# A hybrid attention and retention layer on one core: all values projected first, the pairs' turns written out and overlapped

## The chip, the cores and the metric

The kernel runs on 1 core of one Trainium2 chip. The metric is device time in microseconds (us); the kernel before takes 620.38 us, median of 3 runs (620.24 to 620.57). Engines are named as in the profile: PE (TensorE) with its weight loads PEld, DVE (VectorE), ACT (ScalarE), POOL (GpSimd), and SP, which only issues DMAs here.

## The reference, cut to what matters

```python
h = rmsnorm(x, norm_mix_pre)                        # x: 512 tokens x 1024
proj = h @ w_in                                     # columns qa ka va qr kr vr gr, 512 each
ya = moba_attention(qa, ka, va, rel_bias)           # 8 heads of 64: causal softmax, relative bias
yr = retention(qr, kr, vr, gr)                      # 8 heads of 64: rotary, decay, group norm, gate
x = x + rmsnorm(concat(ya, yr) @ w_out, norm_mix_post)
h = rmsnorm(x, norm_ffn_pre)
u = causal_conv3(h @ w_up)                          # 2 x 2816 columns
x = x + rmsnorm((gelu(u_gate) * u_value) @ w_down, norm_ffn_post)
```

With 512 tokens, blocks of 256 and three blocks allowed, the sparse attention is plain causal attention; retention is computed as scores times a decay mask times values, followed by a normalisation over each head's 64 columns and a gate.

## The kernel before, in words

All matrix products are made of three passes (high by high, high by low, low by high): a weight block of 512 KB is loaded into one of four slots of `raw`, ACT copies it to the high part in `ws` (`split_hi`), DVE subtracts for the low part (`split_lo`; POOL for the first block), and PE uses it. `unit_done` frees a slot. A unit of the input projection is 24 matmuls of 512 columns: 128 output columns (a pair of heads) for all tokens, with the weights stationary, into one bank of PSUM.

The mixer works through four pairs of heads. A turn (`mixer_turn`) projects seven units, kA, qA, vA, kR, qR, vR and gR, each in three steps of eight matmuls, and hangs the attention work between the steps: in the first nine steps (r = 0 to 8) the retention scores of the pair before (`ret_scores`), then in twelve steps (u = 0 to 11) the scores, turned probabilities and products of this pair's softmax attention (`moba_scores`, `moba_turn`, `moba_mix`), and the retention mix and group norm of the pair before (`ret_mix`, `ret_rows`, `ret_turn_out`). Turn 0 is written out with its first two units in halves of 256 tokens, turns 1 to 3 are a loop on every engine, and the retention of the last pair lies inside the output projection (`out_rows`).

Values come out of the projection as columns. ACT copies them to SBUF (`evacuate`, backwards in token order), PE transposes them in four 128 x 128 pieces (`moba_values` L801, `ret_values` L751), and ACT copies the rows out again.

Every engine works through its own list in order; a wait on a semaphore holds what is behind it. The lists that matter here, by function:

- ACT: `exponent` (L1225), `swap_halves` (four copies of 32 rows, L1175), `stack_hi` (L1158, L1160), `split_hi` (L1105), `copy_turned` (L1217), `ret_copy`, squares of the centred rows (L1245).
- DVE: `bias_and_max` (L1648), `normalise` (L1655, L1657), `ret_decay` (L1596), `rotate` (L1666, L1667), `stack_lo` (L1577, L1579), `ret_center` (L1608 to L1612), `ret_variance` (L1617), `ret_norm` (L1621), `ret_gate` (L1626), `ret_low`, `gate_finish`, `split_lo` (L1528).
- POOL: for each pair the bias and decay tables' loads, `double_keys` (L634), `group_rstd(i - 1)` (L620 and the power L622), `rotary_sum(i, 0)` and `(i, 1)` (L626).
- PE: every three-pass matmul has the line of the helper `three`, L694; row transposes L705, the warm-up L723.

In the tail, the x rows 0 and 1, whose space held probabilities, are loaded again before the residual is added; x rows 2 and 3 stay in place. `norm_mix_post` has its half of `gains` from the start; `vA` and `vR` lie in the other half, which `norm_ffn_pre` gets later. The feed-forward part (up projection, convolution and down projection, both with seven products instead of eight for blocks) follows.

Of the kernel before, what the change touches and what calls it, by code (L numbers as in the profile page):

```python
# [36 lines left out]
P = 128  # L37
# [12 lines left out]
GROUPS = [1, 0, 2, 4, 3, 5, 6]  # L50
KA, QA, VA, KR, QR, VR, GR = range(7)
NU = 7
OUT0 = NU * PAIRS
# [78 lines left out]


# [68 lines left out]
def at_turn(f, n, i, per_turn):  # L202

    if isinstance(i, int):
        return f(n + i * per_turn)
    a, b = f(n + per_turn), f(n + 2 * per_turn)
    return (b - a) * i + (2 * a - b)


# [5 lines left out]
def build(nc, x, norm_mix_pre, w_in, rel_bias, w_out, norm_mix_post, norm_ffn_pre, w_up,  # L215
          conv_w, conv_b, w_down, norm_ffn_post, rotary, decay, onehot, out):
    ctx = ExitStack()
    with ctx:
# [46 lines left out]
        vA = gains[:, 0, 0:SEQ]  # L265
        vArow = part(0, 512).rearrange("p (t c) -> p t c", t=ST)
        probs = xs[:, 0:2, :].rearrange("p s (r c) -> p (s r) c", c=SEQ)
        probsT = [part(128 + 1664 * h, 2048).rearrange("p (t c) -> p t c", t=ST) for h in range(2)]
        vR = gains[:, 0, SEQ:2 * SEQ]
        vRrow = part(4096, 512).rearrange("p (t c) -> p t c", t=ST)  # L270
        gate = part(4608, 512)
# [89 lines left out]
        UNIT_BANK = [0, 1, 0, 1, 0, 1, 7]  # L361
        S_BANK, T_BANK, YA_BANK, YR_BANK = (2, 3), (4, 5), 6, 7
        O_BANK = [(0, 1), (5, 6), (2, 3), (4, 7)]
        H_BANK = [(2, 3), (4, 5), (6, 7), (2, 3)] + O_BANK
        UP_BANK = [(0, 1, 5, 6), (2, 3, 4, 7)]
        X_BANK, Y_BANK = [(0, 1), (2, 3), (4, 5)], [6, 7]

# [24 lines left out]
        load_granted, bias_granted = sem("load_granted"), sem("bias_granted")  # L392
# [10 lines left out]
        ident_set = sem("ident_set")  # L403
# [10 lines left out]
        evacuated = sem("evacuated")  # L414
# [4 lines left out]
        vA_turned, vA_ready = sem("vA_turned"), sem("vA_ready")  # L419
# [3 lines left out]
        vR_turned, vR_ready = sem("vR_turned"), sem("vR_ready")  # L423
# [64 lines left out]
        def _(sp):  # L488
# [3 lines left out]
            def load(n, i, per_turn, source, k_major=True):  # L492
                c = slot_of(n)
                if not (isinstance(i, int) and freed_at(n + i * per_turn) == 0):

                    m = n if isinstance(i, int) else n + per_turn
                    last_unit = freed_at(m + (i * per_turn if isinstance(i, int) else 0)) - 1
                    sp.wait_ge(lo_sem(last_unit), at_turn(lambda k: lo_count(freed_at(k) - 1), n, i, per_turn))
                    if not isinstance(i, int):
                        sp.sem_inc(load_granted, 1)  # L500
# [5 lines left out]
            def load_turn(i, j0=0, j1=NU):  # L506
                for j in range(j0, j1):
# [1596 lines left out]
```

## Time and profile before

| | |
|---|---|
| median of the runs | 620.38 us |
| runs | 620.57, 620.38, 620.24 us |
| profiled execution, first to last instruction (its span) | 619.2 us |
| median less that span | 1.2 us |
| mean granted clock | 0.995 |
| PE, PEld busy | 98%, 86% |
| DVE, ACT, POOL busy | 77%, 59%, 23% |

The profiled execution comes with its span alone; the 1.2 us between it and the median are what a run has around its instructions. A matmul's busy time overlaps the next one's, so a busy share of PE tells little, and the distance between two starts is what counts. In the timeline an "x8" row is eight instructions of one form in a row, its first number their start and its second the time until the last one has drained.

### The profile page before, as it was taken

Reading aid. Unit: us, or ns where it says so; the run is one execution under the profiler, and the core shown is the slowest. Engines: PE = TensorE matmul, PEld = TensorE weight load, DVE = VectorE, ACT = ScalarE, POOL = GpSimd, SP = SyncE. Lnnn points to the kernel's source line nnn. Section 1 sums busy time; section 2 is a strip of 40 time slices with the busy share of each in tenths; the row PEclk is TensorE's granted clock in tenths of the full one; section 3 lists DMA queues with packets and bytes.
Section 4 is the critical chain, followed back from the end, with each engine's and each line's share of the span. In section 5 each row is a group of like instructions: output and inputs, shape, how many; then the busy total and the mean of one; then the engine's idle time right before and its main releaser. Section 6 shows DMA issues by size and latency. Waiting matters only on the chain.

```text
span 619.2 us, 9966 instructions
## 1 busy us (share of the span) xinstructions
PE 606.9 (98%) x3710; PEld 532.1 (86%) x3710; DVE 473.9 (77%) x678; ACT 365.0 (59%) x571; POOL 143.9 (23%) x145
## 2 busy tenths in 40 slices
PE   8999999999999999999999999999999999899996
PEld 8888778778787877889989999999999988688885
DVE  3657548656855885978975598888999898999886
ACT  5558338536743853773844566666667655766661
POOL 4313103111310302312021222222222223422213
PEclk9999999999999999999999999999999999899999
DMA  9834223322422254681477988998899879996933
GB/s 275 241 105 127 80 69 103 102 67 68 135 68 68 102 193 157 190 242 35 103 168 145 179 169 163 218 185 177 151 224 192 174 145 180 165 223 168 238 93 136
DMA packets 87785, 93.27 MB, mean 151 GB/s; under 512 B 3049, under 2 KB 72345, under 8 KB 87746
## 3 DMA queue, kind: packets, MB, share of 16 engines
q0 software_dynamic: 26352, 35.15, 33.7%
q1 hardware_dynamic: 61394, 57.59, 29.3%
q8 instruction: 25, 0.41, 0.3%
q14 instruction: 14, 0.11, 0.1%
HBM read 90.62 MB, written 2.12 MB: 150 GB/s over the span
## 4 chain that ended last, share of the span: by engine, by line
PE 84%; DVE 8%; POOL 2%; issue 2%; ACT 2%; DMA 1%; DVEq 0%; SPq 0%; POOLq 0%; ACTq 0%
PE bank L694 75%; PE bank L774 1%; PE bank L836 1%; DVE ws L1940 1%; PE bank L705 1%; DMA gains<-in_norm_mix_pre_dram 1%; POOL grstd L622 1%; PE bank L825 1%; DVE xs L1648 1%; PE bank L765 1%; PE bank L764 1%; POOL work L626 1%; PE bank L815 1%; PE bank L814 1%; DVE work L1818 1%
## 5 line engine op out<-in xcount | busy, mean ns | idle before, releaser
L694 PE MATMUL bank<-hT,ws 128*128 128x256 f32 (+1 forms) x1656 | 295.3, 332 | 0.7 <-DVE work L1626 0.6
L694 PEld LDWEIGHTS bank<-hT,ws 128*128 128x128 f32 x1656 | 245.8, 190 | 28.2 <-issue 2.5
L694 PE MATMUL bank<-yT,ws 128*128 128x256 f32 x864 | 106.8, 283 | 0.0
L694 PEld LDWEIGHTS bank<-yT,ws 128*128 128x128 f32 x864 | 105.2, 192 | 0.2
L694 PE MATMUL bank<-ws,yT 128*128 128x512 f32 x366 | 88.0, 396 | 2.3 <-DVE yT L1916 2.3
L694 PEld LDWEIGHTS bank<-ws,yT 128*128 128x128 f32 x366 | 68.9, 191 | 17.0 <-issue 3.1
L1367 ACT ACTIVATE ws<-raw 128x1024 fp32r<-128x1024 f32 x46 | 48.7, 1059 | 46.1 <-PE bank L694 46.1
L1824 DVE TENSOR_TENSOR ws<-raw,ws 128x1024 fp32r<-128x1024 f32 x46 | 56.1, 1220 | 15.2 <-ACT ws L1367 15.2
L1528 DVE TENSOR_TENSOR ws<-raw,ws 128x1024 fp32r<-128x1024 f32 x47 | 57.5, 1224 | 5.8 <-ACT ws L1105 5.4
L669 POOL DMA_DIRECT2D raw<-in_w_up_dram x27 | 34.7, 1284 | 108.1 <-DVE ws L1824 103.6
L1105 ACT ACTIVATE ws<-raw 128x1024 fp32r<-128x1024 f32 x48 | 50.7, 1058 | 14.8 <-PE bank L694 10.8
L694 PE MATMUL bank<-ws,hT 128*128 128x512 f32 x240 | 55.6, 389 | 0.0
L694 PEld LDWEIGHTS bank<-ws,hT 128*128 128x128 f32 x240 | 44.9, 188 | 9.2
L1824 DVE TENSOR_TENSOR ws<-late,ws 128x1024 fp32r<-128x1024 f32 x21 | 25.6, 1221 | 16.0 <-ACT ws L1367 16.0
L1367 ACT ACTIVATE ws<-late 128x1024 fp32r<-128x1024 f32 x21 | 22.2, 1059 | 21.9 <-PE bank L694 21.4
L1443 ACT ACTIVATE ws<-raw 128x1024 fp32r<-128x1024 f32 (+1 forms) x28 | 26.5, 950 | 14.6 <-PE bank L694 14.6
L1648 DVE CUSTOM_DVE_ANT_0 xs<-bank,work 128x128 f32<-128x128 f32 (+3 forms) x32 | 14.7, 489 | 25.6 <-PE bank L815 25.4
L1940 DVE TENSOR_TENSOR ws<-raw,ws 128x1024 fp32r<-128x1024 f32 (+1 forms) x28 | 30.3, 1083 | 3.3 <-ACT ws L1443 3.3
L1596 DVE TENSOR_TENSOR work<-bank,work 128x512 f32<-128x512 f32 (+3 forms) x32 | 15.5, 489 | 19.9 <-PE bank L765 19.9
L677 POOL DMA_DIRECT2D raw<-in_w_down_dram x16 | 18.5, 1176 | 34.3 <-DVE ws L1940 34.3
L669 POOL DMA_DIRECT2D late<-in_w_up_dram x9 | 11.7, 1297 | 52.8 <-DVE ws L1824 52.8
L1175 ACT ACTIVATE work<-bank 32x512 f32<-32x512 f32 x32 | 18.9, 590 | 8.5 <-PE bank L694 8.1
(174 smaller groups left out, 793.5 us busy)
## 6 DMA issues: line engine op xcount, KB each, us to landing
raw<-in_w_in_dram SPq DMA_DIRECT2D x28, 512.0 KB, 4.1
raw<-in_w_up_dram POOLq DMA_DIRECT2D x27, 512.0 KB, 6.5
raw<-in_w_up_dram SPq DMA_DIRECT2D x23, 512.0 KB, 5.9
raw<-in_w_out_dram SPq DMA_DIRECT2D x16, 512.0 KB, 3.3
late<-in_w_up_dram SPq DMA_DIRECT2D x12, 512.0 KB, 6.0
raw<-in_w_down_dram POOLq DMA_DIRECT2D x12, 512.0 KB, 7.0
late<-in_w_up_dram POOLq DMA_DIRECT2D x9, 512.0 KB, 6.2
raw<-in_w_down_dram SPq DMA_DIRECT2D x9, 512.0 KB, 4.5
```

Source lines behind the costliest of these rows:

```text
L669: pool.dma_start(up_raw(m).rearrange("p (k n) -> p k n", k=4), up_block(UP_ADDS[p], i), accum_op=ALU.add).then_inc(raw_added[raw_slot_of(m ...
L677: pool.dma_start(raw_unit(n), w_block(p, g), accum_op=ALU.add).then_inc(raw_added[c], 16)
L694: return nc.tensor.matmul(dst, st, mv, start=start, stop=stop, skip_group_check=onto)
L1105: nc.scalar.activation(ws[:, c, 0, :], raw[:, c, :], ACT.Copy).then_inc(w_hi, 1)
L1175: ins = nc.scalar.activation(rots[32 * b:32 * b + 32, :], bank[UNIT_BANK[j]][src:src + 32, :], ACT.Copy)
L1367: nc.scalar.activation(ws[:, c, 0, :], up_raw(UP0 + n), ACT.Copy).then_inc(w_hi, 1)
L1443: nc.scalar.activation(ws[:, c, 0, 0:w], raw_unit(n), ACT.Copy).then_inc(w_hi, 1)
L1528: nc.vector.tensor_tensor(ws[:, c, 1, :], raw[:, c, :], f32(ws[:, c, 0, :]), ALU.subtract).then_inc(w_lo, 1)
L1596: nc.vector.tensor_tensor(retp[:, h, packed(mt):packed(mt) + width(mt)], bank[S_BANK[u % 2]][:, 0:width(mt)], dtab[:, h, 0:width(mt)], ALU ...
L1648: nc.vector.tensor_tensor_reduce(out=probs[:, u % 4, 0:w], in0=bank[S_BANK[u % 2]][:, 0:w], in1=btab[:, h, 0:w], scale=-0.125, scalar=3.0e ...
L1824: nc.vector.tensor_tensor(ws[:, c, 1, :], up_raw(UP0 + n), f32(ws[:, c, 0, :]), ALU.subtract).then_inc(w_lo, 1)
L1940: nc.vector.tensor_tensor(ws[:, c, 1, 0:w], raw_unit(n), f32(ws[:, c, 0, 0:w]), ALU.subtract).then_inc(w_lo, 1)
```

## The change

Constants: the units are now 8 blocks of values, then 20 units in a written-out order, three steps each (60 steps), and each pair's attention and retention begin at a fixed step.

```diff
-GROUPS = [1, 0, 2, 4, 3, 5, 6]
-KA, QA, VA, KR, QR, VR, GR = range(7)
-NU = 7
-OUT0 = NU * PAIRS
+GROUPS = [1, 0, 4, 3, 6]
+KA, QA, KR, QR, GR = range(5)
+VALUES = 8
+MIX_UNITS = [(j, i) for i in range(2) for j in (KA, QA, KR, QR, GR)] + [(j, 2) for j in (KA, QA, KR, QR)]
+MIX_UNITS += [(KA, 3), (QA, 3), (KR, 3), (QR, 3), (GR, 2), (GR, 3)]
+IN_AT = {u: VALUES + q for q, u in enumerate(MIX_UNITS)}
+END = {u: 3 * q + 2 for q, u in enumerate(MIX_UNITS)}
+STEPS = 3 * len(MIX_UNITS)
+BLOCKS_FROM = (9, 24, 38, 51)
+RETENTION_FROM = (18, 33, 47, 60)
+OUT0 = VALUES + len(MIX_UNITS)
+OUT_K = (0, 1, 2, 4, 5, 6, 3, 7)
```

Values are projected first, with the activations stationary and 512 value columns moving, so that they come out as rows, for all pairs; they are kept in both halves of `gains` (softmax values) and in the space of x rows 2 and 3 (retention values). The tokens of h are mirrored by transposing with a flipped identity, so keys are stored forwards and queries, gates and the rotary table backwards. The projection's first two units are not halved any more.

```diff
+            def value_rows(n, t, p):
+                side, pair = divmod(n, 4)
+                rows = slice((ST - 1 - t) * P, (ST - t) * P)
+                for kk in range(2):
+                    k, cols = 2 * pair + kk, slice(kk * DMIX, kk * DMIX + DMIX)
+                    ins = three(bank[VALUE_BANK[side][t]][:], hT[:, 0, k, rows], hT[:, 1, k, rows],
+                                ws[:, slot_of(n), 0, cols], ws[:, slot_of(n), 1, cols], p,
+                                pair == 0 and p == 0 and kk == 0, pair == 3 and p == 1 and kk == 1)
+                return ins
...
+            def value_copies(side):
+                act.wait_ge(unit_done, 4 * side + 4)
+                for t in range(ST):
+                    nc.scalar.activation((vA_rows, vR_rows)[side][:, ST - 1 - t, :], bank[VALUE_BANK[side][t]][:],
+                                         ACT.Copy).then_inc(v_rows, 1)
```

PE's order (in each of 61 rounds g):

```diff
+            for g in range(STEPS + 1):
+                if g < STEPS:
+                    project(*MIX_UNITS[g // 3], g % 3)
+                if g == 1:
+                    tables()
+                for i in range(PAIRS):
+                    a, b = g - BLOCKS_FROM[i], g - RETENTION_FROM[i]
+                    if i < PAIRS - 1:
+                        if b in (0, 1, 2, 3):
+                            ret_scores(i, 2 * b)
+                            ret_scores(i, 2 * b + 1)
+                        if b == 5:
+                            ret_mix(i)
+                        if b == 6:
+                            ret_rows(i)
+                        if b == 12:
+                            ret_turn_out(i)
+                    if a in (0, 2, 4, 6):
+                        moba_scores(i, a)
+                        moba_scores(i, a + 1)
+                    if a in (3, 5, 7, 9):
+                        moba_turn(i, a - 3)
+                        moba_turn(i, a - 2)
+                    if a == 11 and i < PAIRS - 1:
+                        moba_mix(i)
```

ACT's and DVE's orders in a round, for i = 0 to 3 (a and b as above), are, cut to names:

```
ACT: halftanh at END[GR]+1; moba_stack at END[KA]+1, END[QA]+1; moba_high a12; ret_copy b6;
     swap KR at END[KR]+1; exponents a1,3,5,7; ret_squares b8; copy_turned a4,6,8,10;
     ret_stack 0 at END[KR]+4; swap QR at END[QR]+1; ret_high b13; ret_stack 1 at END[QR]+4;
     behind all pairs, if g % 3 == 1: split_hi(VALUES + g // 3 + 2)
DVE: gate_finish at END[GR]+1; ret_decay b0..3, two each; moba_stack at END[KA]+1, END[QA]+1;
     bias_and_max a1,3,5,7; rotate KR at END[KR]+1; ret_variance b10; ret_gate b13;
     normalise a2,4,6,8; ret_center b7; moba_low a12; ret_norm b11; ret_stack 0 at END[KR]+4;
     rotate QR at END[QR]+2; ret_low b13; ret_stack 1 at END[QR]+4;
     behind all pairs, if g % 3 == 2: split_lo(VALUES + g // 3 + 2)
```

POOL's order, and the loads of the tail on SP (`load` of block n waits for the low split of block n - 4, its slot's last user):

```diff
                 pool.dma_start(dtab, window(decay.tensor, 2 * i, 2)).then_inc(dtab_loaded, 16)
-                if i:
-                    group_rstd(i - 1)
                 rotary_sum(i, 0)
                 double_keys(ksR, rq_hi, rq_double, i)
                 rotary_sum(i, 1)
+                if i:
+                    group_rstd(i - 1)
             group_rstd(PAIRS - 1)
...
             for n in range(2 * KT):
-                load(OUT0 + n, 0, 0, w_out_v[:, n % KT, :], k_major=False)
+                load(OUT0 + n, w_out_v[:, OUT_K[n] if n < KT else n - KT, :], k_major=False)
                 if n == 3:
                     sp.wait_ge(a_turned, 8 * PAIRS)
                     load_x(0)
                     load_x(1)
+                if n == 4:
+                    sp.wait_ge(a_pv, PAIRS)
+                    sp.dma_start(gains[:, 1, :], norm_mix_post[0].partition_broadcast(P)).then_inc(gains1_loaded, 16)
+                if n == 6:
+                    sp.wait_ge(r_pv, PAIRS)
+                    load_x(2)
+                    load_x(3)
```

The tail: the last pair's softmax product and retention are spread over the first pass of the output projection in pieces of three matmuls, (j, r) being the weight block and the first of three matmuls in it:

```diff
+            order = [(j, 3) for j in range(4)] + [(j, 0) for j in range(4)]
+            order += [(j, r) for j in range(4) for r in (6, 9)] + [(j, r) for j in range(4, KT - 1) for r in (0, 3, 6, 9)]
+            for e, (j, r) in enumerate(order):
...
+                out_rows(0, 12 * j + r, 12 * j + r + 3)
+                if 1 <= e < 9:
+                    ret_scores(last, e - 1)
+                if e == 4:
+                    moba_mix(last)
+                if e == 12:
+                    ret_mix(last)
+                if e == 14:
+                    ret_rows(last)
+                if e == 24:
+                    ret_turn_out(last)
```

and ACT's list there is `split_hi` (third block), `gate_halftanh`, two `copy_turned`, `ret_high`, `split_hi` (fourth block), `moba_high`, two splits, `ret_copy`, two splits, `ret_squares`, split, `ret_high`, split. DVE's is in the same manner, with one split each before the centre, the variance and the norm. The first rows of h, the conv taps and the bias vectors are made as before, the taps and vectors behind the values (`tables` in round 1). The loads at the start are x 0, x 1, `norm_mix_pre`, two value blocks, x 2, x 3, then two more. The loop of turns is gone on every engine.

## Rows read from the trace of the kernel before

**Rows 1.** The page, busy time by engine: busy us, share of the span, instructions.

```profile
PE 606.9 (98%) x3710; PEld 532.1 (86%) x3710; DVE 473.9 (77%) x678; ACT 365.0 (59%) x571; POOL 143.9 (23%) x145
```

**Rows 2.** Waits of PE: releaser, us in total, times, longest.

```profile
PE bank L694 <- DVE yT L1916: 2.3, 1, 2.3
...
PE bank L694 <- DVE work L1626: 0.6, 3, 0.2
```

**Rows 3.** Windows, turn 2 and its stretch of softmax blocks: length, then busy us by engine.

```profile
107.61:160.49 52.88, 52.68 (x269) 41.77 (x268) 35.22 (x70) 29.19 (x58) 9.75 (x10) 1.00 0.31 89
141.20:163.04 21.84, 21.64 (x112) 17.90 (x111) 18.12 (x46) 16.91 (x39) 5.23 (x5) 1.00 0.26 72
```

**Rows 4.** Timeline of PE, turn 2: start us, us until drained, line, operation.

```profile
118.98 0.60 PE L751 MATMUL bank<-ident,gains 128*128 128x128 f32 x4
119.34 0.47 PE L764 MATMUL bank<-qsR,ksR 128*128 128x512 f32 x1
...
119.87 2.00 PE L694 MATMUL bank<-hT,ws 128*128 128x512 f32 x8
```

**Rows 5.** Timeline of PE, first halved unit.

```profile
13.75 3.12 PE L694 MATMUL bank<-hT,ws 128*128 128x256 f32 x24
```

**Rows 6.** Timeline of PE, output projection.

```profile
239.13 6.62 PE L694 MATMUL bank<-ws,yT 128*128 128x512 f32 x28
246.39 0.66 PE L790 MATMUL bank<-ident,work 128*128 128x128 f32 x4 [0.64 <-DVE work L1621]
246.80 19.39 PE L694 MATMUL bank<-ws,yT 128*128 128x512 f32 x84
266.04 1.03 PE L705 MATMUL bank<-ident,work 128*128 128x128 f32 x8
```

**Rows 7.** Timeline of PE, turn 2, steps 8 to 10.

```profile
158.81 2.07 PE L694 MATMUL bank<-hT,ws 128*128 128x512 f32 x8
161.08 2.07 PE L694 MATMUL bank<-hT,ws 128*128 128x512 f32 x8 [0.20 <-DVE work L1626]
...
163.78 0.48 PE L694 MATMUL bank<-hT,ws 128*128 128x512 f32 x1
```

**Rows 8.** Groups of DVE in turn 2, shapes apart: busy us, mean ns, idle before.

```profile
L1528 DVE TENSOR_TENSOR ws<-raw,ws 128x1024 fp32r<-128x1024 f32 x7 | 8.5, 1218 | 0.0
...
L1577 DVE TENSOR_TENSOR yT<-work,ksR 64x512 fp32r<-64x512 f32 x2 | 1.7, 844 | 0.8 <-ACT ksR L1158 0.8
...
L1648 DVE CUSTOM_DVE_ANT_0 xs<-bank,work 128x512 f32<-128x512 f32 x2 | 1.3, 688 | 0.0
...
L1657 DVE TENSOR_SCALAR xs<-xs,rowinv 128x256 f32<-128x256 f32 x2 | 0.7, 353 | 0.1
```

**Rows 9.** Groups of ACT in turn 2.

```profile
L1225 ACT ACTIVATE xs<-xs,negmax 128x512 f32<-128x512 f32 (+3 forms) x9 | 5.1, 572 | 0.2
L1175 ACT ACTIVATE work<-bank 32x512 f32<-32x512 f32 x8 | 4.7, 590 | 2.2 <-PE bank L694 2.2
...
L1158 ACT ACTIVATE ksR<-work 64x512 fp32r<-64x512 f32 x2 | 1.3, 631 | 2.1 <-POOL work L626 2.1
```

**Rows 10.** Timeline of POOL, turn 2: the power and a rotary sum.

```profile
152.98 1.69 POOL L622 TENSOR_TENSOR grstd<-gms,neghalf 128x8 f32<-128x8 f32 x1
154.65 1.29 POOL L626 TENSOR_TENSOR work<-work 128x512 f32<-128x512 f32 x1
```

**Rows 11.** Timeline of all engines, turn 0: POOL and DVE at one time.

```profile
44.97 1.29 POOL L626 TENSOR_TENSOR work<-work 128x512 f32<-128x512 f32 x1 [13.01 <-DVE work L1667]
44.98 1.42 DVE L1657 TENSOR_SCALAR xs<-xs,rowinv 128x256 f32<-128x256 f32 x1
```

**Rows 12.** Window behind the feed-forward wait; the third number from the end is the clock.

```profile
532.00:535.00 3.00, 3.00 (x9) 2.29 (x9) 2.96 (x4) 2.33 (x4) 0.05 (x1) 0.56 1.04 156
```

**Rows 13.** Timeline at the same place, PE's row.

```profile
531.57 4.64 PE L694 MATMUL bank<-ws,yT 128*128 128x512 f32 x13 [2.33 <-DVE yT L1916]
```

**Rows 14.** The page, DMA issues: KB each, us to landing.

```profile
raw<-in_w_out_dram SPq DMA_DIRECT2D x16, 512.0 KB, 3.3
```

More of the change, by code:

```diff
@@ L873, in _ @@
             warm(8)
-            def term(n, p, part, first, last):
-                c = slot_of(n)
-                for k in range(KT):
-                    cols = slice(k * P, (k + 1) * P)
-                    ins = three(bank[n][:, part], ws[:, c, 0, cols], ws[:, c, 1, cols], hT[:, 0, k, part], hT[:, 1, k, part],
-                                p, first and k == 0, last and k == KT - 1)
-                return ins
-            pe.wait_ge(h_hi, 4)
-            pe.wait_ge(w_hi, 1)
-            term(0, 0, FRONT, True, False)
@@ new lines, in exponent, with moba_high @@
+            def exponent(i, u):
+                w = width(moba_block(u)[1])
+                act.wait_ge(a_biased, 8 * i + u + 1)
+                nc.scalar.activation(probs[:, u % 4, 0:w], probs[:, u % 4, 0:w], ACT.Exp, scale=-1.0,
+                                     bias=negmax[:, u:u + 1], accum_out=rowsum[:, u:u + 1]).then_inc(a_exp, 1)
+            def moba_high(i):
+                act.wait_ge(a_pv, i + 1)
+                nc.scalar.activation(yT[:, 0, i, :], bank[YA_BANK][:], ACT.Copy).then_inc(a_yhi, 1)
@@ L1280, in _ @@
+            last = PAIRS - 1
+            split_hi(OUT0 + 2)
+            gate_halftanh(last)
+            copy_turned(last, 6)
+            copy_turned(last, 7)
+            ret_high(last - 1)
+            split_hi(OUT0 + 3)
+            moba_high(last)
+            split_hi(OUT0 + 4)
+            split_hi(OUT0 + 5)
+            ret_copy(last)
             split_hi(OUT0 + 6)
             split_hi(OUT0 + 7)
-            act.wait_ge(r_centered, PAIRS)
-            nc.scalar.activation(squares, centered, ACT.Square).then_inc(r_sq, 1)
+            ret_squares(last)
@@ L1560, in _ @@
             h_low(3)
+            for n in range(3, VALUES + 2):
+                split_lo(n)
             dve.wait_ge(rot_loaded, 16)
@@ L1710, in mixer_turn @@
[L1710 to L1722 removed]
+                    if a in (1, 3, 5, 7):
+                        bias_and_max(i, a - 1)
+                        bias_and_max(i, a)
@@ new lines, in _ @@
+                    if g == END[KR, i] + 1:
+                        rotate(i, KR)
+                    if b == 10:
+                        ret_variance(i)
+                    if b == 13:
+                        ret_gate(i)
+                    if a in (2, 4, 6, 8):
+                        normalise(i, a - 2)
+                        normalise(i, a - 1)
+                    if b == 7:
+                        ret_center(i)
+                    if a == 12:
+                        moba_low(i)
```

636 lines of the change are left out of this document (291 added, 345 removed).

## The prediction

> **What bounds the kernel now.** I read the busy table first [rows 1]: the matrix engine (PE) is busy 98% of 619.2 us, the vector engine (DVE) 77%. Such a PE share only says that matmuls overlap, so I went to start-to-start times. In long runs a 512-column matmul starts every 0.229 us (84 from 246.80 to 266.04 [rows 6]), a 256-column one every 0.125 us (24 in 3.12 us, the last one's drain included [rows 5]). The view of PE's waits [rows 2] is nearly empty: three waits of the gR unit for the gate product of the pair before (L1626) and 2.3 us in the feed-forward part, which the change doesn't touch; the last pair's normed rows add 0.64 (L1621 [rows 6]). So PE's instruction stream sets the time, and a wait added to it adds itself. Then I asked how near the other engines are. One turn takes 52.9 us, with 35.2 us of DVE and 29.2 of ACT; but in the stretch from the first attention scores to the last probabilities, 21.8 us, DVE is busy 18.1 and ACT 16.9 [rows 3]. That is the stretch the change presses together.
>
> **The parts, and what they save.** The profiled span is 619.2 us, the median of the runs 620.4: 1.2 us lie outside the span, and I add them at the end.
>
> Units: 28 before, 28 after, of 24 matmuls of 512 columns each; value rows are as long as column units and have the form (activations stationary, weights moving) of the 84 in [rows 6]. No change in matmul time: 0.
> Value transposes: eight groups of four go. A group takes 0.36 us (118.98 to 119.34) and makes the first matmul behind it about 0.09 later [rows 4]; I take 0.43, so 3.4 us.
> Halved first units: 96 matmuls of 256 columns become 48 of 512: 12.0 - 11.0, at most 1.0; I take 0.8 [rows 5, 6].
> Gate waits: eight matmuls take 2.27 us to the next start (158.81 to 161.08) where 1.84 is usual (2.00 for eight from 119.87 with 0.16 of drain) plus 0.09 behind transposes [rows 4, 7]; three times 0.35: 1.1. The gR unit moves to another bank than the gate product reads, so this goes.
> Normed-rows wait at the end: 28 matmuls take 7.26 us (239.13 to 246.39) for 6.4 plus 0.1 [rows 6]: 0.8; it is taken out here and its successor costed below.
> Saved: 3.4 + 0.8 + 1.1 + 0.8 = 6.1 us. Copies of values (ACT) fall from 16 to 8, and the flips of the token order cost nothing: some access runs backwards either way. The two extra x reloads and the second table come under the tail. The value phase itself I follow from 13.75 us: two weight units (5.4), rows 2 (1), the third unit's front (2.7), rows 3 (1), backs (8.2), five units (27.4) and no wait: about 59.5. Weights are loaded and split a unit ahead; nothing is saved or lost.
>
> **What it presses together.** A turn loses six steps of eight matmuls and the transposes, 52.9 - 6 x 1.84 - 0.9 - 0.4 = 40.7 us, for the same attention work on DVE and ACT. DVE loses two weight splits (1.2 each [rows 8]) of 35.2: 32.8 of 40.7, 81%. On average that fits. But both engines run their lists in order, and now the unit of kR ends just as the scores of the same pair begin (steps 24, 39, 51), so rotation, key stacks, the earlier pair's group norm and eight softmax blocks share the stretch. And on POOL `group_rstd(i-1)` moves behind the second `rotary_sum(i, 1)`: the norm waits for rotation (DVE), then the sum 1.29, then 0.19 + 1.68 for the power [rows 10], 3.3 us with gaps. Before, only the power was in the way, 2.0.
>
> Durations that I use: bias of 512 columns 0.69 each, so the pairs 0.5, 0.8, 1.0, 1.3 by width; normalising pairs with their reciprocals 0.8, 0.9, 1.1, 1.3; split 1.2; stack 1.4 to 1.7 [rows 8]; every other 512-column DVE operation 0.6 to its successor, like the bias: rotate 1.2, centre (three) 1.5, variance, norm, gate, low 0.6, gate finish 1.1; ACT exponent 0.4 to 0.8 with its accumulator, four half swaps 2.4, a stack 1.25, split 1.0 [rows 9].
>
> *Pair 1*, from the end of the retention mix of pair 0 (0). PE: eight matmuls and the rows, scores from 2.3; it could be through with the last turned probabilities (step 33) after 22.6 - 0.35 (the same stretch before, 141.20 to 163.78 [rows 3, 7]) + 1.0 for two retention scores - 0.5: 25.0. ACT and DVE: copy 0.6, swap 3.0, rotate 4.2, centre 5.7, bias 6.2, normalise and split 9.0, bias 9.8. ACT now has two exponents and the key stack, and DVE's next is that stack's low part: 11.6, then 13.0. Variance 13.6, normalise 14.5, rotate 15.7. Next on DVE is the norm: 3.3 for POOL, 19.0, 19.6. Behind it bias 20.6 (PE has waited for the norm since 16.6), split 21.8, gate finish 22.9, normalise 23.9, stack 25.3, gate 25.9, low 27.1 (it waits for ACT's high part), bias 28.4, then ACT: exponents, split and copies 31.1; last turn over at 31.6. Late by 6.6 us.
> *Pair 2*, from the start of step 38. Scores at 4.3, PE could be through at 27.5. Swap 7.3, rotate 8.5, centre, normalise, bias 11.6, split, normalise 13.7, stack 15.6, variance, bias 17.2, rotate 18.4; norm waits until 21.7, 22.3; normalise, split 24.5, bias 25.8; DVE's next is the query stack, which ACT makes behind the exponents, 27.8, 29.2; next pair's keys 30.6, gate, low 32.3, normalise 33.6; turned 34.1. Late by 6.6.
> *Pair 3*, from step 51: the group norm lies apart from the rotation, and the centre comes after the mix. Swap 2.4, rotate 3.6, ..., centre 10.5, bias 11.3, stacks and swap on ACT 15.5, copies 16.5, exponents 18.7, gate finish 20.3, last exponent 26.0, split 27.0, copies 27.8, turned 28.3 against 24.6: 3.7.
> *Tail.* The fourth output weight is split on ACT behind gate, copies and the high part: 2.0 us of waiting in step (3, 3). SP must hold the reloads of x rows 2 and 3 until the last retention mix, and the eighth weight comes after them: landing some 5.9 us after the mix (one w_out load takes 3.3 [rows 14]; for the two x loads of the same size ahead of it I take 1.3 each, between 0 and a whole 3.3). On ACT the squares are queued behind its split, then POOL: the last norm is 2.0 late.
> Added: 0.1 (pair 0) + 6.6 + 6.6 + 3.7 + 4.0 = 21.0 us. 619.2 - 6.1 + 21.0 + 1.2 = 635.3; I say 635.
>
> Bounds. Without any waiting at the head of a list, DVE's work from the first rotation to the last probabilities of pair 1 sums to 20.1 us and begins at 3.0: 23.1, before PE's 25.0, so the least is nothing added. The most is what I have, plus the clock: PE's one idle stretch of over 2 us before (2.3, L1916) was followed by a stretch at a mean granted clock of 0.56 from 532 to 535, that is 1.2 instead of 2.4 GHz for most of it, in which 13 matmuls took 4.64 us instead of 3.1: 1.5 more [rows 2, 12, 13]. The new waits of 3.0, 2.9 and 2.6 us could do so three times: 4.5 more, 640. I take none of it and keep it for the range.
>
> A sum on POOL and a DVE operation collide: a normalising operation of 256 columns took 1.42 us beside POOL's sum, 0.35 is its usual time [rows 8, 11]. The Trainium skill (SBUF — State Buffer, Who interferes with whom) says that a DVE instruction with two SBUF inputs and a GpSimd instruction that reads SBUF exclude each other for a whole instruction. By that rule the splits, too, would meet the sums and key copies that now fall into the pressed stretch, up to about 1 us a pair, 638; by the rows alone I count nothing, as DVE mostly stands still during the sums.
>
> **Rivals.** (a) *The lists keep up* (chance 0.17, faster): the waits at the head of DVE's list fall into its slack. For it: 81% load, and before PE waited 0.35 us a turn with DVE busy 18.1 of 21.8. Against it: these waits follow from the order. It decides if blocked time per pair stays under about 2 us. Time: 620.4 - 6.1 = 614, with a tail of 3: 617.
> (b) *It evens out* (0.05, same): the head waits cost 6 us in all, 619.1 to 621.6.
> (c) *Half of it* (0.10): only the norm's wait and the tail count, 2 x 3 + 4 = 10 less 6.1: 622 to 626.
> (d) *The clock drops too* (0.10): 637 to 643, by one to three of the 1.5 us above and slower power operations.
> (e) *The value phase is starved at the start* (0.05): w1 now comes before x rows 2 and 3, so the third token block is later; one transfer in a queue of them is worth 1 to 2 us, so 620.4 - 6.1 + 21 + 2 = 637.
> The forecast, 626 to 640: 0.53.
>
> **The numbers.** 0.2% (1.2 us) is about what this measurement can tell. Slower 0.78, same 0.05, faster 0.17. Range 619 to 643; the slow case by itself 626 to 640.
>
> **What would show it.** PE idle in front of L790's successor (turning out the normed rows) in pairs 1 and 2 of about 3 and 1.5 us, released by DVE; before the last probabilities' transposes in steps 33 and 47, about 1 and 3 us; DVE idle for POOL's power before the norm, 3 us twice. No value transposes; no matmuls of 256 columns ahead of the feed-forward part. The part behind the mixer as long as before. I am wrong if PE's waits before that part sum to under 6 us: then DVE's list had more room than my chain gives it.

## The result, and the profile after

The changed kernel takes 648.5 us (median of four runs, 647.0 to 649.9) against 620.5 for the kernel before: ratio 1.0446, 95% interval 1.0423 to 1.0468. It is slower, as forecast, but by 28 us and not by 15; 648.5 lies above the range. Two of its four runs took 647.0 and 647.2 us at a mean granted clock of 0.982 and 0.981, two took 649.8 and 649.9 at 0.976, and the profile is that of the run of 647.0, so the account below explains that one and not the last 1.5 us of the median.

The page's busy line and PE's waits of the changed kernel (releaser, us in total, times, longest), beside [rows 1, 2]:

```profile
PE 614.3 (95%) x3630; PEld 532.0 (82%) x3630; DVE 470.2 (73%) x678; ACT 359.2 (56%) x563; POOL 142.5 (22%) x147
```

```profile
PE bank L800 <- DVE work L1661: 8.6, 3, 3.4
PE bank L829 <- ACT work L1252: 4.9, 3, 2.9
PE bank L829 <- DVE xs L1695: 4.4, 2, 2.9
PE bank L708 <- DVE yT L1957: 3.1, 2, 2.3
PE bank L737 <- POOL work L589: 2.5, 1, 2.5
PE bank L708 <- DVE ws L1563: 0.8, 1, 0.8
```

L800 turns out the normed rows, L829 turns the probabilities, L708 is the three-pass matmul; L1661 is the group norm, L1695 the normalising, L1252 the copy of turned probabilities, L1563 a weight's low part. The 2.5 behind L737 is at the start of the kernel, where the warm-up now waits for the flipped identity too; there the kernel before waited 1.8 and, a little later, 1.0. Now the places, PE's timeline (start us, us until drained, line, tile, count, idle before):

```profile
115.50 2.37 PE L784 MATMUL bank<-work,xs 128*64 128x512 f32 x16
...
133.31 0.90 PE L829 MATMUL bank<-ident,xs 128*128 128x128 f32 x4 [1.48 <-DVE xs L1695]
...
139.17 0.66 PE L800 MATMUL bank<-ident,work 128*128 128x128 f32 x4 [3.12 <-DVE work L1661]
...
141.17 3.08 PE L708 MATMUL bank<-hT,ws 128*128 128x512 f32 x8
...
150.81 1.06 PE L829 MATMUL bank<-ident,xs 128*128 128x128 f32 x8 [1.09 <-ACT work L1252]
...
165.15 2.37 PE L784 MATMUL bank<-work,xs 128*64 128x512 f32 x16
...
186.78 0.66 PE L800 MATMUL bank<-ident,work 128*128 128x128 f32 x4 [2.14 <-DVE work L1661]
...
197.85 1.77 PE L829 MATMUL bank<-ident,xs 128*128 128x128 f32 x8 [2.93 <-DVE xs L1695]
...
214.27 2.37 PE L784 MATMUL bank<-work,xs 128*64 128x512 f32 x16
...
238.44 1.35 PE L829 MATMUL bank<-ident,xs 128*128 128x128 f32 x8 [2.88 <-ACT work L1252]
...
256.18 2.37 PE L784 MATMUL bank<-work,xs 128*64 128x512 f32 x16
...
270.77 1.11 PE L800 MATMUL bank<-ident,work 128*128 128x128 f32 x4 [3.37 <-DVE work L1661]
...
302.36 3.88 PE L708 MATMUL bank<-hT,ws 128*128 128x256 f32 x31
```

The L784 rows are the four retention mixes and the last row is the first matmul of the up projection; they serve as milestones below. In the kernel before that matmul started at 275.99:

```profile
275.99 1.24 PE L694 MATMUL bank<-hT,ws 128*128 128x256 f32 x9
```

So the whole loss, 302.36 - 275.99 = 26.4 us, lies ahead of the feed-forward part; behind it stand 342.9 us of span now and 343.2 before. The long waits sit where I said; the 1.48 us at 133.31, ahead of the second two blocks of probabilities in pair 1, were not in the forecast. What I did not put into the sum is the granted clock, the third number from the end here, in windows right behind those waits (length, busy us by engine, clock, DMA share, GB/s):

```profile
140.10:143.40 3.30, 3.30 (x10) 2.60 (x9) 2.96 (x7) 2.99 (x9) 0.00 (x0) 0.50 0.27 73
187.90:191.20 3.30, 3.30 (x10) 2.71 (x11) 2.24 (x5) 1.64 (x5) 0.76 (x1) 0.50 0.38 120
198.20:201.50 3.30, 3.30 (x12) 2.79 (x11) 2.52 (x4) 2.52 (x6) 0.00 (x0) 0.50 0.00 0
239.10:242.40 3.30, 3.30 (x11) 2.72 (x10) 2.79 (x5) 2.87 (x6) 0.00 (x0) 0.50 0.45 159
269.80:276.60 6.80, 5.83 (x16) 4.75 (x17) 4.44 (x5) 2.35 (x3) 0.78 (x2) 0.50 0.70 225
```

Five stretches at 0.50, that is 1.2 GHz, together 20.5 us by the times at which the clock changes; each begins in a wait of PE or within 1.1 us of its end. The eight matmuls at 141.17 take 3.08 us until drained, 2.0 at the full clock [rows 4]. My first account was therefore simple: saved 6.1, waits about 21 as forecast, and 20.5 us at half the clock for some 10 more. It adds up to 25, near the 26.4, and the runs below show that all three of its terms are wrong.

### The profile page after: what moved, and what is told of

Read it like the earlier page. It is cut to its first block, busy times and chain, and to the rows that moved or that the text cites. A ratio compares the mean times of both kernels' runs of the same rounds, so it can differ in the third digit from the quotient of the medians.

```text
span 645.2 us, 9451 instructions
## 1 busy us (share of the span) xinstructions
PE 614.3 (95%) x3630; PEld 532.0 (82%) x3630; DVE 470.2 (73%) x678; ACT 359.2 (56%) x563; POOL 142.5 (22%) x147
## 4 chain that ended last, share of the span: by engine, by line
PE 74%; DVE 13%; ACT 5%; issue 3%; DMA 2%; POOL 1%; DVEq 0%; SPq 0%; POOLq 0%; ACTq 0%
PE bank L708 67%; PE bank L784 1%; PE bank L841 1%; DVE ws L1981 1%; ACT xs L1260 1%; DMA gains<-in_norm_mix_pre_dram 1%; PE bank L719 1%; PE bank L829 1%; DVE ws L1563 1%; DVE xs L1686 1%; DVE yT L1616 1%; DMA raw<-in_w_out_dram 1%; POOL grstd L637 1%; ACT work L1211 1%; DVE xs L1695 1%
## 5 line engine op out<-in xcount | busy, mean ns | idle before, releaser
L708 PE MATMUL bank<-hT,ws 128*128 128x256 f32 (+1 forms) x1416 | 249.6, 332 | 0.2 <-DVE hT L1581 0.2
L708 PEld LDWEIGHTS bank<-hT,ws 128*128 128x128 f32 x1416 | 210.8, 192 | 23.0 <-issue 1.1
L708 PE MATMUL bank<-yT,ws 128*128 128x256 f32 x864 | 106.8, 283 | 0.0
L708 PEld LDWEIGHTS bank<-yT,ws 128*128 128x128 f32 x864 | 105.2, 192 | 0.2
L708 PE MATMUL bank<-ws,hT 128*128 128x512 f32 x432 | 99.9, 390 | 0.0
L708 PE MATMUL bank<-ws,yT 128*128 128x512 f32 x366 | 91.0, 405 | 3.9 <-DVE yT L1957 3.1
L708 PEld LDWEIGHTS bank<-ws,hT 128*128 128x128 f32 x432 | 80.8, 188 | 16.5
L708 PEld LDWEIGHTS bank<-ws,yT 128*128 128x128 f32 x366 | 70.2, 195 | 19.9 <-issue 3.3
L1563 DVE TENSOR_TENSOR ws<-raw,ws 128x1024 fp32r<-128x1024 f32 x47 | 58.7, 1250 | 34.5 <-ACT ws L1130 33.8
L1865 DVE TENSOR_TENSOR ws<-raw,ws 128x1024 fp32r<-128x1024 f32 x46 | 56.2, 1222 | 14.7 <-ACT ws L1402 14.6
L1260 ACT ACTIVATE xs<-xs,negmax 128x128 f32<-128x128 f32 (+3 forms) x32 | 17.7, 555 | 34.4 <-DVE negmax L1686 34.3
L691 POOL DMA_DIRECT2D raw<-in_w_down_dram x16 | 18.5, 1176 | 34.3 <-DVE ws L1981 34.3
L829 PE MATMUL bank<-ident,xs 128*128 128x128 f32 x80 | 14.1, 303 | 9.5 <-ACT work L1252 4.9
```

Source lines behind the costliest of these rows:

```text
L691: pool.dma_start(raw_unit(n), w_block(p, g), accum_op=ALU.add).then_inc(raw_added[c], 16)
L708: return nc.tensor.matmul(dst, st, mv, start=start, stop=stop, skip_group_check=onto)
L829: ins = nc.tensor.transpose(bank[T_BANK[u % 2]][:, t * P:(t + 1) * P], probs[:, u % 4, t * P:(t + 1) * P], ident[:])
L1260: nc.scalar.activation(probs[:, u % 4, 0:w], probs[:, u % 4, 0:w], ACT.Exp, scale=-1.0, bias=negmax[:, u:u + 1], accum_out=rowsum[:, u:u + ...
L1563: nc.vector.tensor_tensor(ws[:, c, 1, :], raw[:, c, :], f32(ws[:, c, 0, :]), ALU.subtract).then_inc(w_lo, 1)
L1865: nc.vector.tensor_tensor(ws[:, c, 1, :], up_raw(UP0 + n), f32(ws[:, c, 0, :]), ALU.subtract).then_inc(w_lo, 1)
```

## The experiments

All times are medians; the kernel before was at 620.3 to 621.1 beside them. E1 to E4 each change one thing in the changed kernel.

**E1, the power first.**

```diff
                 double_keys(ksR, rq_hi, rq_double, i)
+                if i in (1, 2):
+                    group_rstd(i - 1)
                 rotary_sum(i, 1)
-                if i:
+                if i == 3:
                     group_rstd(i - 1)
```

> The changed kernel, with POOL's power of the pair before (pairs 1 and 2 of the loop) issued ahead of the rotary sum of the queries, as the kernel before had it. Theory A (in-order lists): POOL no longer waits for the rotation and the 1.3 us sum, so the waits ahead of turning out the normed rows of pairs 0 and 1 (3.12 and 2.14 us) shrink by 1.5 to 3 us each, and with them the half-clock stretches that begin behind them; 1 to 4 us of this come back as longer waits for the last probabilities, as DVE's list is only shifted. Time 641 to 646 against 648.5. Rival B (DVE and ACT are simply too busy in the pressed stretch, the order doesn't matter): the wait moves whole to the last probabilities, 648 to 649.

643.8 us (ratio 1.037, 1.0355 to 1.0384), 4.7 less: theory A.

**E2, the last x reload behind the eighth weight.**

```diff
-                if n == 6:
+                if n == 7:
                     sp.wait_ge(r_pv, PAIRS)
                     load_x(2)
                     load_x(3)
```

> The changed kernel, with the second reload of x (its wait for the last retention mix, and its two transfers) behind the load of the eighth output weight. Theory A: ACT's split no longer waits 4.2 us for that weight, so squares, variance, power and norm of the last pair come 3 to 4 us earlier, the 3.37 us wait ahead of the last turning out is gone, and the 6.8 us at half the clock that begin there go too. Time 641 to 645. Rival B: the wait belongs to the chain of the last group norm itself (squares, reduce, two POOL operations, norm), which remains: 648 less at most 1.

643.0 us (1.0351, 1.0336 to 1.0367), 5.5 less: theory A. In the changed kernel ACT stood idle for that weight ahead of the last squares:

```profile
264.79 1.06 ACT L1130 ACTIVATE ws<-raw 128x1024 fp32r<-128x1024 f32 x1 [4.19 <-DMA raw<-in_w_out_dram]
265.75 0.61 ACT L1229 ACTIVATE work<-work 128x512 f32<-128x512 f32 x1
```

**E3, ACT's retention stacks ahead of exponents and copies.**

```diff
                         swap_halves(i, KR)
+                    if g == END[KR, i] + 4:
+                        ret_stack(i, 0)
+                    if g == END[QR, i] + 4:
+                        ret_stack(i, 1)
                     if a in (1, 3, 5, 7):
...
-                    if g == END[KR, i] + 4:
-                        ret_stack(i, 0)
...
-                    if g == END[QR, i] + 4:
-                        ret_stack(i, 1)
```

> The changed kernel, with ACT's retention key and query stacks ahead of the exponents and copies of their step instead of behind them. Theory A: DVE stands still at its key stack for about 2 us in pairs 1 to 3 while ACT does two exponents first; without it the waits for the last probabilities shrink by about 1 us a pair, but the exponents come 1.3 us later, which may give it back: 644 to 648. Rival B (density alone): only the order of two pieces of ACT work changes, 648 to 649.5.

640.2 us (1.0311, 1.0297 to 1.0325), 8.3 less: nearly twice the most that I gave it, the largest of the three, from ACT's stacks trading places with exponents: the 1.98 us that DVE stood before its key stack in pair 1 (row at 130.38 below) are gone. (Its profile is of a run of 645.0, the slowest of six, the rest being 639.0 to 640.9, so it shows less than the gain.)

**E4, the waits filled with matmuls.** This one adds work and reads nothing of it; it tells the wait from the clock.

```diff
+            def fill(b, n):
+                for m in range(n):
+                    nc.tensor.matmul(bank[b][:], hT[:, 0, 0, 0:P], hT[:, 0, 0, :], start=True, stop=True)
+
             def ret_turn_out(k):
+                if k != 2:
+                    pe.wait_ge(r_centered, k + 1)
+                    fill(YR_BANK, (12, 9, 0, 14)[k])
                 pe.wait_ge(r_normed, k + 1)
...
                 qt = moba_block(u)[1]
+                if i == 2 and u == 6:
+                    pe.wait_ge(aq_lo, 7)
+                    fill(0, 12)
+                if i == 3 and u == 6:
+                    pe.wait_ge(cos_done, 8)
+                    fill(1, 12)
```

> The changed kernel with work added: in front of the five longest waits of PE (turning out the normed rows of pairs 0, 1 and 3, the last probabilities of pairs 2 and 3) stand 12, 9, 14, 12 and 12 matmuls of 512 columns whose result nobody reads, into a bank that is free there, 2.0 to 3.2 us each, about as long as the wait. It separates the wait from the clock. Theory A (the idle waits are what lowers the clock, and 20.5 us at half of it cost some 10 us): the half-clock stretches are gone and the time falls to 637 to 641 although 59 matmuls were added. Rival C (the clock falls for another reason, the total load for instance, and would fall with more work all the same): time 648 to 652.

643.0 us (1.0376, 1.035 to 1.0402): 59 more matmuls, 5.5 us less. The idle waits do take the clock with them: the mean granted clock of the span rises from 0.982 to 0.998 and nothing at half of it is left ahead of the kernel's end. But the gain is about half of what theory A asked. The milestones and one of the filled places, with what follows it, show why:

```profile
115.81 2.38 PE L784 MATMUL bank<-work,xs 128*64 128x512 f32 x16
...
136.21 2.88 PE L799 MATMUL bank<-hT 128*128 128x512 f32 x12
139.50 0.66 PE L807 MATMUL bank<-ident,work 128*128 128x128 f32 x4 [0.41 <-DVE work L1674]
...
148.88 0.47 PE L772 MATMUL bank<-qsR,ksR 128*128 128x512 f32 x1 [0.64 <-DVE negmax L1699]
...
151.15 1.06 PE L842 MATMUL bank<-ident,xs 128*128 128x128 f32 x8 [1.11 <-ACT work L1265]
...
165.48 2.37 PE L784 MATMUL bank<-work,xs 128*64 128x512 f32 x16
...
213.19 2.37 PE L784 MATMUL bank<-work,xs 128*64 128x512 f32 x16
...
254.58 2.37 PE L784 MATMUL bank<-work,xs 128*64 128x512 f32 x16
...
298.34 1.84 PE L708 MATMUL bank<-hT,ws 128*128 128x256 f32 x14
```

From mix 0 to mix 1 PE needs 49.67 us at the full clock and 49.65 in the changed kernel with 3.4 us at half of it: no difference. PE ran faster from 140 to 143 and then waited 0.64 and more for DVE. Where DVE's list sets the pace, slow matmuls only fill time in which PE would have waited. In the profiled executions the clock costs 302.36 - 298.34 = 4.0 us, 2.4 of them behind the last mix (46.18 against 43.76), where PE sets the pace. The medians are 5.5 apart, as half of the changed kernel's runs had a still lower mean clock.

**E5, the three edits together.**

> The three edits of the first runs together (POOL's power first, the last x reload behind the eighth weight, ACT's retention stacks first), nothing else. Theory A (each removes its own wait): the gains of 4.7, 5.5 and 8.3 us add up to 630 to 633. Rival B (they removed the same half-clock stretches and the same slack more than once): 636 to 639.

629.9 us (1.0147, 1.0129 to 1.0166), 18.6 less: the three gains add up (18.5), theory A. No stretch at half the clock is left ahead of the kernel's end, although PE still waits three times for 2.3 to 3.0 us, as long as where the clock fell before. The length of a wait alone doesn't say whether the clock falls; the last section comes back to it.

**E6, norm, turning out and gate of pairs 0 and 1 later.**

```diff
-                        if b == 12:
+                        if b == (14, 14, 12)[i]:
                             ret_turn_out(i)
...
-                    if b == 11:
+                    if b == (13, 13, 11, 11)[i]:
                         ret_norm(i)
...
-                    if b == 13:
+                    if b == (15, 15, 13, 13)[i]:
                         ret_gate(i)
```

(the high and low parts move with the gate)

> The kernel with the three edits, and for pairs 0 and 1 the norm, the turning out and the gate product two steps later in the lists of DVE, PE and ACT (steps 13, 14 and 15 after the retention begins, not 11, 12 and 13). Theory A: the rest of the waits ahead of turning out (DVE's norm behind POOL's power) goes in pairs 0 and 1, and DVE no longer stands at the head of its list for it, so the last probabilities come earlier too; 3 to 6 us less than the kernel with the three edits alone. Rival B (DVE's and ACT's total work in the stretch is the limit): at most 1 us less.

626.0 us (1.0081, 1.0065 to 1.0097), 3.9 less: theory A.

**E7, the last probabilities of pairs 1 and 2 turned a step later**, on top of E6.

```diff
-                    if a in (3, 5, 7, 9):
+                    if a in (3, 5, 7) or a == 9 + late:
```

(`late` is 1 for pairs 1 and 2; copies, mix and split likewise)

> On top of the kernel with the later norm: in pairs 1 and 2 the last two probabilities are turned one step (eight matmuls, 1.84 us) later, and the copies, the attention mix and its split with them. Theory A (latency of the lists): 1 to 2 us of waiting in each of the two pairs is covered by matmuls, and a wait under about 1 us no longer takes the clock with it: 2 to 5 us less. Rival B (density): the wait moves a step on, to the next pair's first scores or its first probabilities, no gain.

626.7 us (1.0095, 1.0068 to 1.0122), no gain: rival B's time, but not for its reason. What E7 was to cover was no longer there. E5's trace has 1.10 and 2.96 us of waiting for the last probabilities of pairs 1 and 2, E6's has none of over 0.2, so the later norm had already removed both. What is new in E7's trace is a longer wait at the same pair's retention scores (0.48 in E6), where DVE's decay is late:

```profile
146.18 0.44 PE L774 MATMUL bank<-qsR,ksR 128*128 128x384 f32 x1 [1.69 <-DVE work L1640]
```

Just ahead of that decay DVE itself stood still for 0.70 us, waiting for ACT at the gate's low part. So this wait, too, speaks for the order of the lists and not for density.

**E8, softmax first on DVE**, on top of E6: `ret_norm(i - 1)` right behind the bias of pair i's last two blocks, pair 3's query stack one step later.

> On top of the kernel with the three edits and the later norm (626.0): DVE does the bias of the last two blocks of each pair before the norm of the pair before, and in pair 3 before the low part of the query stack as well. In the trace of that kernel two waits of PE are left in the mixer: 3.05 us for the last probabilities of pair 3, whose bias came 4 us after its scores, behind variance, normalising, query stack and norm on DVE; and 1.98 us for the normed rows of pair 1, whose norm stood behind two stacks on DVE. Theory A (order in DVE's list): both go, 621 to 623. Rival B (DVE's total): they come back behind another operation, 625 to 626.

623.7 us (1.0033, 1.0018 to 1.0048), 2.3 less: mostly theory A, a little short of its time.

**E9, the fourth output weight first**, on top of E8.

```diff
-            ret_high(last - 1)
             split_hi(OUT0 + 3)
+            ret_high(last - 1)
```

(on DVE its low part ahead of the first decay)

> On top of that, ACT and DVE split the fourth output weight ahead of the last-but-one pair's high part and ahead of the first decay; PE waited 1.9 to 2.1 us for its low part. Theory A: that wait goes, and with it nearly all that the new order had cost: 1.5 to 2.5 us less again, 618.5 to 621, level with the kernel before or a little under it (620.4 less 6.1 saved, plus some 3 to 5 of small waits that remain). Rival B: the first retention scores of pair 3 (their decay is now 1.2 us later) wait instead, no gain. Rival D (my saved 6.1 us were never there, the order costs nothing because nothing was saved): no waits left and still 622 or more.

622.1 us (1.0015, 1.0000 to 1.0030), 1.5 less, the low end of theory A's gain; its range of times was missed by 1.

**E10, DVE trimmed at the end of the mixer**, on top of E9: pair 0's turning out and gate a step later; on DVE the query stack of pair 3 stands behind the softmax, ahead of the third and fourth output weights, and the gate finish and gate product of pair 2 behind them.

> On top of the last one: pair 0 turns its normed rows out one step later (its 1.14 us wait), and DVE's query stack of pair 3, gate finish and gate product of pair 2 move behind the softmax and the two output weights (waits of 1.28 us for the last probabilities and 1.52 us for the fourth weight). In the stretch from 214 to 228 us of the last trace DVE never stood still, so theory B (here DVE's total is the limit, not its order) has its one place here: the wait moves to the gate or the decays, 621 to 622.5. Theory A: 3 to 4 us of waits go, 618 to 620.

621.05 us (1.000, 0.9988 to 1.0013): level with the kernel before, and theory B's time. DVE is busy 11.4 of 12 us here (E10, windows), and PE waits 1.4 us for the gate finish at 225.38:

```profile
213.00:225.00 12.00, 10.45 (x53) 7.82 (x51) 11.38 (x24) 7.78 (x15) 1.86 (x2) 1.00 0.36 131
```

**E11, gate in one DVE operation; query stacks 1 and 2 later**, on top of E10. The half that is left out here goes into the gate product, which stays one operation.

```diff
-                nc.vector.tensor_scalar(gate, gate, 0.5, 0.5, ALU.mult, ALU.add).then_inc(gate_sigmoid, 1)
-                dve.wait_ge(gate_sigmoid, k + 1)
-                nc.vector.tensor_tensor(gate[:, ::-1], unit_bank(GR, k)[:], gate[:, ::-1], ALU.mult).then_inc(gate_ready, 1)
+                nc.vector.scalar_tensor_tensor(gate[:, ::-1], gate[:, ::-1], 1.0, unit_bank(GR, k)[:],
+                                               ALU.add, ALU.mult).then_inc(gate_ready, 1)
...
-                    if g == END[QR, i] + 4 and i != 3:
+                    if g == END[QR, i] + (4, 5, 5, 99)[i]:
                         ret_stack(i, 1)
```

> On top of the last one: one DVE operation less for each gate (tanh plus one, times the projection; the half goes into the gate product), 1.1 us of DVE become about 0.7, once in each pair; and the query stacks of pairs 1 and 2 one step later. Theory B (in the stretch around 214 to 226 us DVE's total is the limit): two gates finish there, so 0.8 us of the 1.57 us wait for the gate goes; the 0.6 us wait for pair 2's last probabilities goes with the later stack. Time 619 to 620.3. Against it: the stretch is by now limited by ACT's splits and copies, 620.7 to 621.5.

623.3 us (1.004, 1.0027 to 1.0054), 2.2 more: a miss by my own edit. Pair 2's query stack is needed one step after the place I gave it, and PE now waits for it; the clock falls behind that wait, and the score matmul there, 0.48 until drained in E13, takes 0.79:

```profile
184.24 0.79 PE L774 MATMUL bank<-qsR,ksR 128*128 128x512 f32 x1 [3.38 <-DVE qsR L1619]
```

**E12, the kernel before with the same fused gate.**

> The kernel before with the same fused gate, as a control: there PE waited for the gate only through the 0.35 us in front of the gR unit's bank three times, and DVE had slack. Expected within 0.5 us of the kernel before: 620 to 621. If it gains more than 1 us, the fused gate and not the order would explain a gain of the other kernel.

620.3 us (0.9986, 0.9973 to 0.9998): as expected.

**E13, pair 2's stack put back**, otherwise E11.

> The last variant of the changed kernel with one thing put back: the query stack of pair 2 on DVE again one step earlier. In that variant's trace PE waited 3.4 us for this stack before the retention scores of pair 2, and 3.4 us at half the clock began there (1.7 us more). Theory A: both go and the small wait for pair 2's last probabilities (0.6 us) is back: 623.3 less 5.1 plus 0.6 = 618.8, under the kernel before. If instead the order had saved nothing (the 6.1 us of removed work aren't there), the time stays at 621 or above.

619.6 us (0.9983, 0.9974 to 0.9991): 3.7 less than E11 and 1.2 (0.17%) under the kernel before, though 0.8 above theory A's figure, and 0.6 under E12, which the two intervals don't tell apart. With less DVE work in E10's full place, the wait for the gate finish is 0.5 and no longer 1.4. Its waits of over 0.2 us ahead of the feed-forward part, without the one at the start, and its milestones:

```profile
PE bank L831 <- DVE xs L1698: 0.7, 2, 0.4
PE bank L710 <- DVE ws L1565: 0.5, 1, 0.5
PE bank L710 <- DVE work L1609: 0.5, 1, 0.5
PE bank L802 <- DVE work L1662: 0.3, 1, 0.3
```

```profile
157.18 2.37 PE L786 MATMUL bank<-work,xs 128*64 128x512 f32 x16
...
198.08 2.38 PE L786 MATMUL bank<-work,xs 128*64 128x512 f32 x16
...
234.50 2.38 PE L786 MATMUL bank<-work,xs 128*64 128x512 f32 x16
...
274.82 2.44 PE L710 MATMUL bank<-hT,ws 128*128 128x256 f32 x19
```

## Why the prediction was wrong in size and right in kind

The direction was right, and so was the mechanism, lists worked through in order that make PE wait. What failed is the step "The most is what I have, plus the clock": the waits of 21.0 us, added up from four chains and taken for the most, measured 26.9. The clock, allowed for in the range but put at nothing in the sum, measured 4.0, and 4.6 us were saved instead of 6.1. The waits alone miss by more than the other two terms together.

E13 has the changed kernel's matmuls and few of its waits, E4 has its waits at the full clock. Start to start, E13 has 3.4 us of waits left ahead of the feed-forward part (0.8, 0.9, 1.3 and 0.4 in the four stretches from mix 0 on), so a changed kernel without waits would be there at 274.8 - 3.4 = 271.4. That splits the 26.4 us:

| stretch of PE | changed | E4, full clock | E13 | wait at full clock | forecast |
|---|---|---|---|---|---|
| start to mix 0 | 115.5 | 115.8 | 115.1 | 0.7 | 0.1 |
| mix 0 to mix 1 | 49.7 | 49.7 | 42.1 | 8.4 | 6.6 |
| mix 1 to mix 2 | 49.1 | 47.7 | 40.9 | 7.7 | 6.6 |
| mix 2 to mix 3 | 41.9 | 41.4 | 36.4 | 6.3 | 3.7 + 2.0 |
| mix 3 to feed-forward | 46.2 | 43.8 | 40.3 | 3.8 | 2.0 |
| sum | 302.4 | 298.3 | 274.8 | 26.9 | 21.0 |

The wait is the E4 column less E13's, plus what E13 still waits. Up to 0.6 of the 26.9 may be E4's filling where it was longer than the wait. The kernel before, with 1.9 us of waits counted in the same way, would be at 274.1 without them; saved are 274.1 - 271.4 + 1.9 = 4.6. Then 276.0 - 4.6 + 26.9 + 4.0 = 302.3.

*Saved, forecast 6.1, measured 4.6.* The savings are there (E13), 1.5 short. About 0.5 of it is the start: the first product of the projection begins at 14.22 in E13 and at 13.75 before [rows 5] (13.96 in the changed kernel's own profile). Which term holds the rest was not traced; the value phase itself ends at 59.4, as forecast.

*Waits, forecast 21.0, measured 26.9: the term that failed.* The long waits were in the right places, and all but the fourth output weight (2.0 forecast, 1.9 in E4) were too low. Pair 1's chain shows how (DVE, with POOL's part below it):

```profile
122.89 0.76 DVE L1650 TENSOR_SCALAR gneg<-gsum 128x8 f32<-128x8 f32 x1
...
130.38 1.70 DVE L1616 TENSOR_TENSOR yT<-work,ksR 64x512 fp32r<-64x512 f32 x2 [1.98 <-ACT ksR L1199]
...
134.23 0.68 DVE L1705 TENSOR_TENSOR work<-work,rot 128x512 f32<-128x512 f32 x1
138.42 0.69 DVE L1661 TENSOR_TENSOR work<-work,grstd 128x512 f32<-128x512 f32 x1 [3.51 <-POOL grstd L637]
```

```profile
122.35 1.28 POOL L641 TENSOR_TENSOR work<-work 128x512 f32<-128x512 f32 x1 [8.86 <-DVE work L1705]
...
135.06 1.28 POOL L641 TENSOR_TENSOR work<-work 128x512 f32<-128x512 f32 x1 [2.51 <-DVE work L1705]
...
136.71 1.68 POOL L637 TENSOR_TENSOR grstd<-gms,neghalf 128x8 f32<-128x8 f32 x1
```

Counted from the end of mix 0 (115.50 + 2.37 = 117.87), the centre ends at 6.4 where I had 5.7, the key stack starts at 12.5 where I had 11.6, the norm at 20.5 where I had 19.0, and the last probabilities are turned at 33.8 where I had 31.6. The largest single piece is a collision that I had counted as nothing. The centre's small middle operation, on 8 columns, took 0.17 us all four times in the kernel before. Here it starts while POOL's rotary sum runs (122.35 to 123.63), takes 0.76 and ends with the sum. Pair 2 has the same (0.78), so DVE's lists are some 1.2 us longer by it. The rest of pair 1's lateness is many small pieces: a key stack of 1.7 where I took 1.4, DVE's wait of 1.98 ahead of it where I had 1.8, and 3.5 us between rotation and norm where I had 3.3. That these pieces are the missing 5.9 us is argued, not tested. At the end ACT stood 4.19 us for the last weight (E2) where I had the last norm 2.0 late; E2 alone takes the last stretch from 46.2 to 40.4.

*The clock, forecast 0 in the sum and at most 4.5 in the range, measured 4.0: the second term.* "The new waits of 3.0, 2.9 and 2.6 us could do so three times" was too few: it happened at five waits, and once for 6.8 us. That the price still lies within the 4.5 is luck, two errors that cancel: more stretches than I had, each costing less than my 1.5. I took none of it into the sum, though the trace before showed it behind a wait of 2.3 [rows 2, 12, 13]. The other error would have been to take all of it. The Trainium skill (TensorE: Matmul & The Clock Gate, HAM oscillation — how this bites in real kernels) works out the price of such stretches as their length times one half. By that rule 20.5 us cost 10.2, an estimate; E4 shows 4.0, so here it is an upper bound, and the measurement decides.

*Small slips.* A turn less its steps and transposes is 40.6 us and not 40.7, on which nothing hangs. The 1.2 us outside the span came from a profile and a median of different runs; wherever a run is listed with its own span, the changed kernel's four included, 1.8 lie outside.

*The rivals.* (a), the lists keep up, is refuted as the order stood, yet E3 and E5 show how near it was: four edits of order (E1 to E3, E6) bring 22.5 of the 28 us back. DVE was found nearly full in one place alone, the end of the mixer (E10). (b) and (c), 6 and 10 us of waiting, are refuted by the 26.9. (d), waits plus clock, is the case that came true, and its price of 637 to 643 was too low since the waits in it were. (e), a starved value phase, did not happen: mix 0 comes at 115.5 in the changed kernel and at 115.1 in E13.

*What would show it* held: L800 waits 3.12 and 2.14 us in pairs 1 and 2 (3 and 1.5 forecast), L829 1.09 and 2.93 (1 and 3), DVE waits 3.51 for the power, and the part behind the mixer is as long as before.

## What to carry to other kernels

When overlapping two chains of work takes matmuls out from between them, add up each engine's list in order, not its load, with what another engine does beside it: at 81% average load the order alone cost over 20 us, and an exchange of pieces of ACT work 8. Before covering a wait, look for it in the trace of the kernel that you change; E7 covered one that the edit before had removed. If PE gains idle waits, put the clock into the sum, but price it where PE sets the pace; ahead of a wait that another engine's list will cause anyway, half the clock was free here (mix 0 to mix 1). And fill the waits with idle matmuls once: it costs one run and separates the two.

## What was unexpected of the hardware

The clock does not follow from the length of one wait: waits of 2.1 to 3.4 us were followed or accompanied by half the clock in the changed kernel, and three of 2.3 to 3.0 us in E5 were not. One and the same wait, for pair 3's last probabilities, stands in E6 (2.88 us) and in E7 (2.87 us, ending at 225.06). In E6 the six matmuls behind it run at the full clock, in E7 at half of it:

```profile
223.01 1.06 PE L831 MATMUL bank<-ident,xs 128*128 128x128 f32 x8 [2.88 <-ACT work L1254]
223.83 1.64 PE L710 MATMUL bank<-ws,yT 128*128 128x512 f32 x6
```

```profile
226.01 2.91 PE L710 MATMUL bank<-ws,yT 128*128 128x512 f32 x6
```

E7 has another such stretch about 1 us behind the wait of 1.69 that ends at 146.18, shorter than any that did it in the changed kernel. What decides it stays open. From mix 1 to mix 2 E11 took 45.0 us, with one wait of 3.4 and one such stretch of 3.4, and E13 40.9. Of the 4.1 between them, 3.0 are the longer wait (3.6 for 0.6, start to start), which leaves 1.1 for the clock.

DVE and POOL collided as in [rows 11], not only at the centre but, where the power comes first, on the norm too: 0.69 us alone (138.42 above), and in E5 1.78 beside POOL's rotary sum. E5's rows of DVE and of POOL:

```profile
132.61 1.78 DVE L1663 TENSOR_TENSOR work<-work,grstd 128x512 f32<-128x512 f32 x1 [0.17 <-POOL grstd L637]
```

```profile
132.56 1.28 POOL L641 TENSOR_TENSOR work<-work 128x512 f32<-128x512 f32 x1
```

The norm takes 1.09 us longer, and the sum had 1.23 to go when it began, which fits what the Trainium skill (SBUF — State Buffer, Who interferes with whom) says of a DVE operation with two inputs in SBUF. So the early power of E1 has a price of its own, 1.1 us of DVE in pair 1 of E5.
